# Expert weights in a ring of five places, and the last body's order

## The chip, the cores and the metric

The kernel runs on one core of one Trainium2 chip. Its time is the device time of one execution in microseconds, as the median of several. A separate execution was recorded by the hardware profiler; all durations below come from that one.

## The reference, cut to what matters

One decoder layer on 512 tokens of width 1024, all in float32. First an attention branch and a gated linear attention branch are computed and merged into the residual stream `h`. The last stage, which the change touches, is a mixture of 32 experts, in 4 groups of 8; each token goes to the best two experts of its best group:

```
for g in range(N_GROUPS):
    hg = jax.nn.silu(jnp.einsum('nd,edf->nef', xn, w_gate[g])) * jnp.einsum('nd,edf->nef', xn, w_up[g])
    y = y + jnp.einsum('nef,efd->nd', hg * combine[:, g, :, None], w_down[g])
return h + y_ffn
```

Each expert has a gate matrix (1024 x 256), an up matrix (1024 x 256) and a down matrix (256 x 1024). Each of these 96 matrices is 1024 KB and is read from HBM once.

## The kernel before, in words

**The stages.** The first part of the kernel (up to about 403 us) computes both branches, the router and the choice of experts. Its order is a list written out by hand (`SCHEDULE`). Then comes the expert stage, a loop over rounds; with these inputs there is one round. A round has 8 bodies (`BODIES`), a body has two pairs of experts (side s = 0 and s = 1), so body i holds pairs 2i and 2i+1, that is experts 4i to 4i+3. Each expert gets 64 slots (`SLOT`) for tokens; the two experts of a pair sit side by side in the 128 partitions.

**TensorE's order in a body** (`for i in range(BODIES)` in the tensor block): the gate and up products of pair 2i (`expert_gate_up(i, 0, ...)`, line 1023), those of pair 2i+1, then the down products of the body before (`down(i - 1, n - 1)`, line 1037, both sides), the transposes of the hidden rows (`hidden`, line 1031), the transposes of the gathered rows of the next body (`row_transposes`, line 1017), and the scatter of the body before (`scatter`, line 1110: one-hot products that spread the rows into 8 banks, which VectorE adds to `h`). Bodies 0 and 1 differ: body 0 does its own down products and body 1 does none. Body 7, the last, starts with the down products of body 6, then its own gate and up products, then the scatter of body 6; it ends with its own down products and a last scatter (`last_scatter`, line 1048). ScalarE takes the silu (`hs`, line 1542) and copies the down products (`high_rows`, line 1533), VectorE multiplies (`hg`, line 1997) and subtracts (`low_rows`, line 1970).

**The weights in SBUF.** `w_pair[s]` holds for side s one pair: 2 experts x (gate, up, down). So gate and up of four experts and the down matrices of four experts have a place (96 KB of each partition). The 16 KB at the start of the arena hold in the stage before `xnT` (two buffers of 4 KB, the transposed rows for the router) and `xs` (two buffers of 4 KB, the scaled rows on their way to `rows_hbm`, from which GpSimd gathers the experts' rows); in the expert stage this space is unused.

**The queue of the weights.** All weights are loaded by SyncE (SP) with `dma_start`, in the order of its program, on one hardware queue. SP waits for the semaphore that frees a place (`s_gu[s]`: gate and up products of side s done; `s_down[s]`: down products done) and issues the loads of that pair. The order of the 1024 KB loads, counted as pieces from the first, is: 1 to 5 the gate and up of pair 0 and one down matrix of it (issued at 340 us, when the last merged rows are split); three stores of scaled rows; 6 to 10 the gate and up of pair 1 and one down of it; 11 its other down; the fourth store (`store_rows(NB - 1)`, 512 KB); 12 the other down of pair 0; then `bodies_after_first`: gate and up of pairs 2 and 3 (13 to 20), down of pair 2 (21, 22), gate and up of pairs 4 and 5 (23 to 30), down of pair 3 (31, 32). From body 2 on a body asks for 8 gate and up pieces and 4 down pieces: 33 to 44, 45 to 56, 57 to 68, 69 to 80. At the end come gate and up of pair 14 (81 to 84), down of pairs 12 and 13 (85 to 88), gate and up of pair 15 (89 to 92), down of pairs 14 and 15 (93 to 96). One semaphore per side counts gate and up loads (`s_wgu`), one per side the down loads (`s_wd`).

**The gathers.** For body j GpSimd waits (once) until the four stores of scaled rows have landed, then, body by body, for the row numbers of side s, and issues an indirect DMA on a queue of its own (line 2144).

Of the kernel before, what the change touches and what calls it, by code (L numbers as in the profile page):

```python
# [28 lines left out]
P = 128  # L29
NB = T // P  # L30
KT = D // P
# [7 lines left out]
NG, EPG, FF = 4, 8, 256  # L39
# [6 lines left out]
PAIRS = NE // 2  # L46
BODIES = PAIRS // 2


# [216 lines left out]
def layer_kernel(nc, x, meta_tokens, norm1_w, w_in, q_norm_w, k_norm_w, attn_sinks, gla_gate_up, gla_gate_bias,  # L266
                 gla_norm_w, w_attn_branch, w_gla_branch, w_out, norm2_w, router_rows, norm2_rows,
                 expert_w_gate, expert_w_up, expert_w_down, table, triangle, rows_hbm, out):
    with ExitStack() as ctx:
# [89 lines left out]
        def more(name, shape, dt=F32):  # L359
# [66 lines left out]
        w_pair = [at(f"w_pair{s}", WE + 6 * s * 8 * K1, [P, 2, 3, KT * FF]) for s in range(2)]  # L426
        we = [[[w_pair[s][:, j, i, :].rearrange("p (k n) -> p k n", k=k) for i, k in enumerate((KT, KT, 2))]
               for j in range(2)] for s in range(2)]
        onehot_r = at("onehot_r", WE + 40 * K1, [P, NB, 2 * P], F32R)
# [102 lines left out]
        s_ylo = sem2("y_lo_ready")  # L532
        s_wgu = sem2("gate_up_loaded")
        s_wd = sem2("down_loaded")
# [75 lines left out]
        def slots(j, s):  # L610

            c = 32 * (j % 2) + 16 * s
            return tiles[W_BANK][:, c:c + 8]

        def scatter_bank(i, u):
# [12 lines left out]
        def _(pe):  # L628
# [373 lines left out]
            with pe.Fori(0, rounds) as r:  # L1002
# [17 lines left out]
                def expert_gate_up(i, s, part):  # L1020
                    for k in range(4 * part, 4 * part + 4):
                        for j in range(2):
                            last = nc.tensor.matmul(tiles[GU_BANK[s]][j * SLOT:(j + 1) * SLOT, :].rearrange("p (f n) -> p f n", f=2),  # L1023
                                                    xgT[:, k, s * P + j * SLOT:s * P + (j + 1) * SLOT],
                                                    w_pair[s][:, j, 0:2, k * FF:(k + 1) * FF],
                                                    start=(k == 0), stop=(k == KT - 1))
                    return last
# [6 lines left out]
                def expert_down(s, half):  # L1034
                    for f in range(2):
                        for j in range(2):
                            last = nc.tensor.matmul(tiles[DOWN_BANKS[s][half]][j * SLOT:(j + 1) * SLOT, :],  # L1037
                                                    hT[s][:, f, j * SLOT:(j + 1) * SLOT],
                                                    we[s][j][2][:, f, half * 512:(half + 1) * 512],
                                                    start=(f == 0), stop=(f == 1))  # L1040
                    return last
# [73 lines left out]
                for i in range(BODIES):  # L1115
                    n = r * BODIES + i

                    if i + 1 == BODIES:
                        down(i - 1, n - 1)
                    pe.wait_ge(s_xgT[0], n + 1)  # L1120
                    pe.wait_ge(s_wgu[0], 64 * n + 64)
                    expert_gate_up(i, 0, 0)
                    pe.wait_ge(s_xgT[1], n + 1)
                    expert_gate_up(i, 0, 1).then_inc(s_gu[0], 1)
                    if i == 0:
                        first_slot_weights()
                        for s in range(2):
                            pe.wait_ge(s_ohT[s], n + 1)
                        onehot_transposes(1)
                    pe.wait_ge(s_xgT[2], n + 1)  # L1130
                    pe.wait_ge(s_xgT[3], n + 1)
                    pe.wait_ge(s_wgu[1], 64 * n + 64)
                    expert_gate_up(i, 1, 0)
# [46 lines left out]
        def _(sp):  # L1180
# [17 lines left out]

            def load(pair, s, gate_up, slots=(0, 1)):
                for j in slots:  # L1200
                    e = pair * 2 + j
                    for i, w in ((0, expert_w_gate), (1, expert_w_up)) if gate_up else ((2, expert_w_down),):
                        src = w[0].rearrange("g e a n -> (g e) a n")[bass.ds(e, 1), :, :]
                        src = src.rearrange("o (p k) n -> p (o k) n", p=P) if gate_up else \
                            src.rearrange("o (k p) n -> p (o k) n", p=P)
                        sp.dma_start(we[s][j][i][:, :, :], src).then_inc((s_wgu if gate_up else s_wd)[s], 16)

            def next_gate_up(i, n, sides=(0, 1)):

                for s in sides:  # L1210
                    sp.wait_ge(s_gu[s], n)
                    load(2 * i + s, s, True)

            def next_down(i, n, sides=(0, 1)):

                for s in sides:
                    sp.wait_ge(s_down[s], n)
                    load(2 * i + s, s, False)

            def bodies_after_first(n):  # L1220

                next_gate_up(1, n + 1)
                next_down(1, n + 1, (0,))
                next_gate_up(2, n + 2)
                next_down(1, n + 1, (1,))
                with sp.Fori(2, BODIES - 2) as i:
                    next_gate_up(i + 1, n + i + 1)
                    next_down(i, n + i)
                last = BODIES - 1
                next_gate_up(last, n + last, (0,))  # L1230
                next_down(last - 1, n + last - 1)
                next_gate_up(last, n + last, (1,))
                next_down(last, n + last)

            sp.wait_ge(s_mlo, KT)
            load(0, 0, True)
            load(0, 0, False, (0,))
            def store_rows(b):
# [5 lines left out]
            sp.wait_ge(*banks.emptied(("unit", WO + 1, NB - 1)))  # L1244
            load(1, 1, True)
            load(1, 1, False, (0,))
            sp.wait_ge(s_sq2, 4 * NB)
            load(1, 1, False, (1,))
            store_rows(NB - 1)
            sp.wait_ge(s_pick[3], 1)  # L1250
            sp.wait_ge(s_cast, 2)
            load(0, 0, False, (1,))
            bodies_after_first(0)
            sp.wait_ge(s_rounds, 1)
            rounds = sp.value_load(rounds_i[0:1, 0:1], min_val=1, max_val=T // SLOT)
            with sp.If(rounds > 1):
                with sp.Fori(1, rounds) as r:
                    next_gate_up(0, r * BODIES)
                    next_down(0, r * BODIES)
                    bodies_after_first(r * BODIES)  # L1260
            for u in range(2 * NB):
# [8 lines left out]
        def _(act):  # L1270
# [252 lines left out]
            with act.Fori(0, rounds) as r:  # L1523
# [12 lines left out]
                for i in range(BODIES):  # L1536
                    n = r * BODIES + i
                    if i + 1 == BODIES:
                        high_rows(n - 1)
                    for s in range(2):  # L1540
                        act.wait_ge(s_gu[s], n + 1)
                        nc.scalar.activation(hs[s][:, :], tiles[GU_BANK[s]][:, 0:FF], ACT.Silu).then_inc(s_silu[s], 1)  # L1542
                        if s == 0 and i == 0:
                            onehot_out(1, n + 1)
# [19 lines left out]
        def _(dve):  # L1564
# [371 lines left out]
            with dve.Fori(0, rounds) as r:  # L1936
# [52 lines left out]
                for i in range(BODIES):  # L1989
                    n = r * BODIES + i  # L1990
                    if i + 1 == BODIES:
                        low_rows(n - 1)
                    dve.wait_ge(s_pw, n + 1)
                    for s in range(2):
                        dve.wait_ge(s_silu[s], n + 1)

# [206 lines left out]
```

## Time and profile before

| | us |
|---|---|
| median of 3 runs (663.23 to 665.02) | 663.85 |
| the profiled execution, its own time | 663.98 |
| its span, first to last instruction | 662.2 |
| TensorE busy in the span | 639.2 (97%) |
| hardware queue q1, share of 16 DMA engines over the span | 53.3% |

The span is shorter than the time by 1.8 us, which lie before the first and behind the last instruction. Busy shares are means over stages: the expert stage is the last 259 us, and it is the only one in which the DMA engines are full. TensorE's granted clock is 0.997 of full speed over the span, so no stage of it runs at the lower level.

### The profile page before, as it was taken

How to read it: one execution, taken by the hardware profiler on the slowest of the kernel's cores; microseconds unless marked ns; L12 is line 12 of the kernel's file. 1: busy time of each engine (PE TensorE's matmuls, PEld its weight loads, DVE VectorE, ACT ScalarE, POOL GpSimd, SP SyncE). 2: the span in 40 equal slices, each digit the busy share in tenths (PEclk: the TensorE clock that was granted, in tenths of full speed). 3: DMA queues.
4: the chain of work that ended last, by engine and by line, in shares of the span. 5: the costliest groups of instructions: out<-in, count | busy, mean ns of one | idle time of the engine just before them, and what ended most of it. 6: DMA issues, size and time to landing. Idle time of an engine off the chain costs nothing.

```text
span 662.2 us, 10015 instructions
## 1 busy us (share of the span) xinstructions
PE 639.2 (97%) x3887; PEld 461.9 (70%) x3887; DVE 390.9 (59%) x721; ACT 213.7 (32%) x436; POOL 110.7 (17%) x168
## 2 busy tenths in 40 slices
PE   5799999999999999999989999999999999999998
PEld 3579999998787878778789996345454454635355
DVE  4648335688997979776674667435253443526145
ACT  6346222224444343422534565200101010111112
POOL 3300006799500000000000010111010101010001
PEclk9899999999999999999999999999999999999999
DMA  7442222302232221111454067999999999999933
GB/s 248 150 127 65 64 65 70 120 4 64 65 89 82 83 64 66 64 64 63 149 194 198 33 257 287 419 414 413 418 410 419 409 421 410 420 410 414 414 128 127
DMA packets 49794, 138.78 MB, mean 210 GB/s; under 512 B 6202, under 2 KB 28235, under 8 KB 41556
## 3 DMA queue, kind: packets, MB, share of 16 engines
q1 hardware_dynamic: 47298, 134.44, 53.3%
q0 software_dynamic: 2304, 3.64, 1.5%
q8 instruction: 31, 0.51, 0.3%
q14 instruction: 15, 0.12, 0.1%
q10 hardware_dynamic: 146, 0.07, 0.0%
HBM read 138.69 MB, written 4.19 MB: 216 GB/s over the span
## 4 chain that ended last, share of the span: by engine, by line
PE 85%; DMA 6%; DVE 4%; ACT 2%; issue 2%; POOL 0%; SPq 0%; ACTq 0%; DVEq 0%
PE bank L1023 16%; PE bank L632 13%; PE bank L633 12%; PE bank L634 12%; PE bank L1037 8%; PE bank L1110 6%; DMA w_pair<-in_expert_w_up 3%; DMA w_pair<-in_expert_w_down 2%; PE bank L1017 1%; PE bank L874 1%; PE bank L976 1%; PE bank L1048 1%; PE bank L907 1%; PE bank L942 1%; ACT whi L1313 1%
## 5 line engine op out<-in xcount | busy, mean ns | idle before, releaser
L1023 PE MATMUL bank<-w_pair,xgT 128*64 128x512 f32 x512 | 112.0, 594 | 1.6 <-DMA w_pair<-in_expert_w_up 1.6
L1023 PEld LDWEIGHTS bank<-w_pair,xgT 128*64 128x64 f32 x512 | 37.3, 137 | 70.0 <-issue 69.2
L1635 DVE TENSOR_TENSOR wlo<-wraw,whi 128x2048 fp32r<-128x2048 f32 (+1 forms) x25 | 56.4, 2257 | 20.0 <-ACT whi L1313 20.0
L632 PE MATMUL bank<-whi,xhi 128*128 128x256 f32 x224 | 64.4, 288 | 0.0
L634 PE MATMUL bank<-whi,xlo 128*128 128x256 f32 x224 | 62.9, 281 | 0.0
L633 PE MATMUL bank<-wlo,xhi 128*128 128x256 f32 x224 | 62.9, 281 | 0.0
L632 PE MATMUL bank<-xhi,whi 128*128 128x512 f32 x152 | 62.3, 410 | 0.0
L1037 PE MATMUL bank<-w_pair,hT 128*64 128x512 f32 x256 | 56.7, 593 | 4.2 <-DMA w_pair<-in_expert_w_down 3.1
L633 PE MATMUL bank<-xlo,whi 128*128 128x512 f32 x152 | 60.1, 395 | 0.0
L634 PE MATMUL bank<-xhi,wlo 128*128 128x512 f32 x152 | 59.7, 393 | 0.0
L1997 DVE SCALAR_TENSOR_TENSOR hg<-bank,pair_w,hs 128x256 f32<-128x256 f32 x16 | 7.7, 484 | 84.0 <-ACT hs L1542 84.0
L1313 ACT ACTIVATE whi<-wraw 128x2048 fp32r<-128x2048 f32 (+1 forms) x25 | 46.7, 1872 | 24.9 <-PE bank L641 11.1
L1982 DVE TENSOR_TENSOR h<-h,bank 128x512 f32<-128x512 f32 x64 | 42.0, 683 | 9.6 <-PE bank L1110 8.2
L1970 DVE TENSOR_TENSOR y_lo<-bank,y_hi 128x512 fp32r<-128x512 f32 x32 | 20.6, 686 | 44.7 <-ACT y_hi L1533 44.7
L1037 PEld LDWEIGHTS bank<-w_pair,hT 128*64 128x64 f32 x256 | 18.8, 137 | 39.4 <-issue 37.2
L2036 POOL TENSOR_TENSOR pause<-pause 128x1 f32<-128x1 f32 x34 | 8.8, 270 | 222.8 <-PE bank L1017 119.6
L1110 PE MATMUL bank<-y_hi,onehotT 128*128 128x512 f32 x112 | 44.3, 396 | 0.0
L1110 PE MATMUL bank<-y_lo,onehotT 128*128 128x512 f32 x112 | 43.7, 390 | 0.0
L632 PEld LDWEIGHTS bank<-whi,xhi 128*128 128x128 f32 x224 | 42.1, 188 | 1.8 <-issue 1.4
L634 PEld LDWEIGHTS bank<-whi,xlo 128*128 128x128 f32 x224 | 42.2, 188 | 0.0
L633 PEld LDWEIGHTS bank<-wlo,xhi 128*128 128x128 f32 x224 | 42.1, 188 | 0.0
L1542 ACT ACTIVATE hs<-bank 128x256 f32<-128x256 f32 x16 | 6.1, 383 | 99.5 <-PE bank L1023 99.5
(333 smaller groups left out, 1301.9 us busy)
## 6 DMA issues: line engine op xcount, KB each, us to landing
w_pair<-in_expert_w_gate SPq DMA_DIRECT2D x32, 1024.0 KB
w_pair<-in_expert_w_up SPq DMA_DIRECT2D x32, 1024.0 KB
w_pair<-in_expert_w_down SPq DMA_DIRECT2D x32, 1024.0 KB, 20.4
wraw<-in_w_in SPq DMA_DIRECT2D x17, 1024.0 KB, 5.5
wraw<-in_w_out SPq DMA_DIRECT2D x4, 1024.0 KB, 5.1
h<-in_x SPq DMA_DIRECT2D x4, 512.0 KB, 5.1
wraw<-in_w_gla_branch SPq DMA_DIRECT2D x2, 1024.0 KB, 5.2
wraw<-in_w_attn_branch SPq DMA_DIRECT2D x2, 1024.0 KB, 5.1
```

What stands on the lines that cost most here:

```text
L632: nc.tensor.matmul(ps, lhi(k), rhi(k), start=(k == 0), stop=False)
L633: nc.tensor.matmul(ps, lhi(k), rlo(k), start=False, stop=False)
L634: last = nc.tensor.matmul(ps, llo(k), rhi(k), start=False, stop=(k == kt - 1))
L1023: last = nc.tensor.matmul(tiles[GU_BANK[s]][j * SLOT:(j + 1) * SLOT, :].rearrange("p (f n) -> p f n", f=2), xgT[:, k, s * P + j * SLOT:s * ...
L1037: last = nc.tensor.matmul(tiles[DOWN_BANKS[s][half]][j * SLOT:(j + 1) * SLOT, :], hT[s][:, f, j * SLOT:(j + 1) * SLOT], we[s][j][2][:, f, ...
L1110: last = nc.tensor.matmul(scatter_bank(i, u)[:, :], onehotT[i % 3][s][:, b, :], part[s][:, cols_], start=(s == 0 and part is y_hi), stop=( ...
L1313: nc.scalar.activation(wh, raw, ACT.Copy).then_inc(s_hi, 1)
L1635: nc.vector.tensor_tensor(wl, raw, wh.bitcast(F32), ALU.subtract).then_inc(s_lo, 1)
L1970: last = nc.vector.tensor_tensor(y_lo[s][:, cols_], tiles[DOWN_BANKS[s][half]][:, :], y_hi[s][:, cols_].bitcast(F32), ALU.subtract)
L1982: nc.vector.tensor_tensor(h[:, b, cols_], h[:, b, cols_], scatter_bank(i, u)[:, :], ALU.add).then_inc(s_add[u % 4], 1)
L1997: nc.vector.scalar_tensor_tensor(hg[s][:, :], tiles[GU_BANK[s]][:, FF:2 * FF], pair_w[:, 2 * i + s:2 * i + s + 1], hs[s][:, :], ALU.mult, ...
L2036: return nc.gpsimd.tensor_tensor(o, a, b, op)
```

## The change

Gate and up move out of `w_pair` into a ring of five places (`w_ring`): four are the gate and up parts of `w_pair`, the fifth is `w_fifth`, 16 KB at the start of the arena. Expert e goes to place e % 5, each place has a semaphore of its own, and a pair waits for its two experts' places. The down matrices stay where they were. After the gate and up products of pair p SP loads experts 2p+5 and 2p+6. The order of SP's program changes with it: expert 4's gate is issued behind the last logits and ahead of the fourth store, its up behind a wait for the third and fourth store to land; in body 0 both pairs of down matrices (2 and 3) are asked for ahead of the gate and up of pairs 4 to 6; in body 7 nothing but down matrices is left to load. The loop on SP is unrolled.

In body 7 TensorE does the gate and up products of pair 14 ahead of the down products of body 6; ScalarE's `high_rows` and VectorE's `low_rows` of body 6 move between the two sides accordingly.

```diff
--- before.py
+++ after.py
@@ -45,6 +45,7 @@
+RING = 5
@@ -424,8 +425,9 @@
         y_lo = [more(f"y_lo{i}", [P, D], F32R) for i in range(2)]
         assert place[0] <= 80 * K1, place[0] / K1
         w_pair = [at(f"w_pair{s}", WE + 6 * s * 8 * K1, [P, 2, 3, KT * FF]) for s in range(2)]
-        we = [[[w_pair[s][:, j, i, :].rearrange("p (k n) -> p k n", k=k) for i, k in enumerate((KT, KT, 2))]
-               for j in range(2)] for s in range(2)]
+        wd = [[w_pair[s][:, j, 2, :].rearrange("p (k n) -> p k n", k=2) for j in range(2)] for s in range(2)]
+        w_fifth = at("w_fifth", 0, [P, 2, KT * FF])
+        w_ring = [w_pair[s][:, j, 0:2, :] for s in range(2) for j in range(2)] + [w_fifth[:, :, :]]
         onehot_r = at("onehot_r", WE + 40 * K1, [P, NB, 2 * P], F32R)
         assert WE + 44 * K1 <= G + 48 * K1
         def view(t, rows, groups):
@@ -530,7 +532,7 @@
         s_down = sem2("down_done")
         s_yhi = sem2("y_hi_ready")
         s_ylo = sem2("y_lo_ready")
-        s_wgu = sem2("gate_up_loaded")
+        s_ring = [sem(f"gate_up{k}_loaded") for k in range(RING)]
         s_wd = sem2("down_loaded")
         s_sc = [sem(f"scatter_bank{i}_full") for i in range(4)]
         s_add = [sem(f"scatter_bank{i}_added") for i in range(4)]
@@ -611,6 +613,10 @@
 
             c = 32 * (j % 2) + 16 * s
             return tiles[W_BANK][:, c:c + 8]
+
+        def ring_loads(n, e):
+
+            return 32 * (n * len(range(e % RING, NE, RING)) + e // RING + 1)
 
         def scatter_bank(i, u):
 
@@ -1022,7 +1028,7 @@
                         for j in range(2):
                             last = nc.tensor.matmul(tiles[GU_BANK[s]][j * SLOT:(j + 1) * SLOT, :].rearrange("p (f n) -> p f n", f=2),
                                                     xgT[:, k, s * P + j * SLOT:s * P + (j + 1) * SLOT],
-                                                    w_pair[s][:, j, 0:2, k * FF:(k + 1) * FF],
+                                                    w_ring[(4 * i + 2 * s + j) % RING][:, :, k * FF:(k + 1) * FF],
                                                     start=(k == 0), stop=(k == KT - 1))
                     return last
 
@@ -1036,7 +1042,7 @@
                         for j in range(2):
                             last = nc.tensor.matmul(tiles[DOWN_BANKS[s][half]][j * SLOT:(j + 1) * SLOT, :],
                                                     hT[s][:, f, j * SLOT:(j + 1) * SLOT],
-                                                    we[s][j][2][:, f, half * 512:(half + 1) * 512],
+                                                    wd[s][j][:, f, half * 512:(half + 1) * 512],
                                                     start=(f == 0), stop=(f == 1))
                     return last
 
@@ -1115,13 +1121,14 @@
                 for i in range(BODIES):
                     n = r * BODIES + i
 
-                    if i + 1 == BODIES:
-                        down(i - 1, n - 1)
                     pe.wait_ge(s_xgT[0], n + 1)
-                    pe.wait_ge(s_wgu[0], 64 * n + 64)
+                    for e in (4 * i, 4 * i + 1):
+                        pe.wait_ge(s_ring[e % RING], ring_loads(r, e))
                     expert_gate_up(i, 0, 0)
                     pe.wait_ge(s_xgT[1], n + 1)
                     expert_gate_up(i, 0, 1).then_inc(s_gu[0], 1)
+                    if i + 1 == BODIES:
+                        down(i - 1, n - 1)
                     if i == 0:
                         first_slot_weights()
                         for s in range(2):
@@ -1129,7 +1136,8 @@
                         onehot_transposes(1)
                     pe.wait_ge(s_xgT[2], n + 1)
                     pe.wait_ge(s_xgT[3], n + 1)
-                    pe.wait_ge(s_wgu[1], 64 * n + 64)
+                    for e in (4 * i + 2, 4 * i + 3):
+                        pe.wait_ge(s_ring[e % RING], ring_loads(r, e))
                     expert_gate_up(i, 1, 0)
                     expert_gate_up(i, 1, 1).then_inc(s_gu[1], 1)
                     if 2 <= i < BODIES - 1:
@@ -1196,45 +1204,51 @@
             for c in range(2, NCHUNK):
                 load_w(c)
 
-            def load(pair, s, gate_up, slots=(0, 1)):
+            def rows_of(w, e, **by):
+                return w[0].rearrange("g e a n -> (g e) a n")[e, :, :].rearrange(by.pop("as_"), **by)
+
+            def load_gate(e, both=True):
+                sp.dma_start(w_ring[e % RING][:, 0, :].rearrange("p (k n) -> p k n", k=KT),
+                             rows_of(expert_w_gate, e, as_="(p k) n -> p k n", p=P)).then_inc(s_ring[e % RING], 16)
+                if both:
+                    load_up(e)
+
+            def load_up(e):
+                sp.dma_start(w_ring[e % RING][:, 1, :].rearrange("p (k n) -> p k n", k=KT),
+                             rows_of(expert_w_up, e, as_="(p k) n -> p k n", p=P)).then_inc(s_ring[e % RING], 16)
+
+            def load_down(pair, slots=(0, 1)):
                 for j in slots:
...
-            def next_gate_up(i, n, sides=(0, 1)):
-
-                for s in sides:
-                    sp.wait_ge(s_gu[s], n)
-                    load(2 * i + s, s, True)
-
...
-            def bodies_after_first(n):
-
-                next_gate_up(1, n + 1)
-                next_down(1, n + 1, (0,))
-                next_gate_up(2, n + 2)
-                next_down(1, n + 1, (1,))
-                with sp.Fori(2, BODIES - 2) as i:
-                    next_gate_up(i + 1, n + i + 1)
-                    next_down(i, n + i)
-                last = BODIES - 1
-                next_gate_up(last, n + last, (0,))
-                next_down(last - 1, n + last - 1)
-                next_gate_up(last, n + last, (1,))
-                next_down(last, n + last)
+                    sp.dma_start(wd[pair % 2][j][:, :, :],
+                                 rows_of(expert_w_down, 2 * pair + j, as_="(k p) n -> p k n", p=P)).then_inc(s_wd[pair % 2], 16)
+
+            def next_gate_up(pair, n):
+
+                sp.wait_ge(s_gu[pair % 2], n + pair // 2 + 1)
+                for e in (2 * pair + RING, 2 * pair + RING + 1):
+                    if e < NE:
+                        load_gate(e)
+
+            def next_down(pair, n):
+
+                sp.wait_ge(s_down[pair % 2], n + pair // 2 + 1)
+                load_down(pair + 2)
+
+            def rest_of_round(n):
+
+                for i in range(BODIES):
+                    for pair in (2 * i, 2 * i + 1):
+                        if pair + 2 < PAIRS:
+                            next_gate_up(pair, n)
+                    if i != 1:
+                        done = i if i == 0 else i - 1
+                        for pair in (2 * done, 2 * done + 1):
+                            next_down(pair, n)
 
             sp.wait_ge(s_mlo, KT)
-            load(0, 0, True)
-            load(0, 0, False, (0,))
+            for e in range(2):
+                load_gate(e)
+            load_down(0, (0,))
             def store_rows(b):
                 sp.wait_ge(s_xs_loc[b], 1)
                 sp.dma_start(rows_hbm[b * P:(b + 1) * P, :], xs[b % 2][:, :]).then_inc(s_xsd[b], 16)
@@ -1242,22 +1256,33 @@
             for b in range(NB - 1):
                 store_rows(b)
             sp.wait_ge(*banks.emptied(("unit", WO + 1, NB - 1)))
-            load(1, 1, True)
-            load(1, 1, False, (0,))
+            for e in range(2, 4):
+                load_gate(e)
+            load_down(1, (0,))
             sp.wait_ge(s_sq2, 4 * NB)
-            load(1, 1, False, (1,))
+            load_down(1, (1,))
+            sp.wait_ge(*banks.filled(("logits", NB - 1)))
+            load_gate(4, False)
             store_rows(NB - 1)
             sp.wait_ge(s_pick[3], 1)
             sp.wait_ge(s_cast, 2)
-            load(0, 0, False, (1,))
-            bodies_after_first(0)
+            load_down(0, (1,))
+            for b in (NB - 2, NB - 1):
+                sp.wait_ge(s_xsd[b], 16)
+            load_up(4)
+            rest_of_round(0)
...
@@ -1535,9 +1560,9 @@
 
                 for i in range(BODIES):
                     n = r * BODIES + i
-                    if i + 1 == BODIES:
-                        high_rows(n - 1)
                     for s in range(2):
+                        if s == 1 and i + 1 == BODIES:
+                            high_rows(n - 1)
                         act.wait_ge(s_gu[s], n + 1)
                         nc.scalar.activation(hs[s][:, :], tiles[GU_BANK[s]][:, 0:FF], ACT.Silu).then_inc(s_silu[s], 1)
                         if s == 0 and i == 0:
@@ -1988,10 +2013,10 @@
                 next_onehots(2)
                 for i in range(BODIES):
                     n = r * BODIES + i
-                    if i + 1 == BODIES:
-                        low_rows(n - 1)
                     dve.wait_ge(s_pw, n + 1)
                     for s in range(2):
+                        if s == 1 and i + 1 == BODIES:
+                            low_rows(n - 1)
                         dve.wait_ge(s_silu[s], n + 1)
 
                         nc.vector.scalar_tensor_tensor(hg[s][:, :], tiles[GU_BANK[s]][:, FF:2 * FF], pair_w[:, 2 * i + s:2 * i + s + 1],
```

## Rows read from the trace of the kernel before

**Rows 1.** DMA and engines by stretch; last columns granted clock, DMA share, GB/s.
```profile
389.00:404.00 15.00, 14.88 (x129) 14.48 (x130) 11.97 (x36) 10.11 (x24) 2.40 (x3) 1.00 1.01 410
404.00:408.00 4.00, 4.00 (x20) 1.29 (x18) 3.44 (x19) 3.80 (x10) 0.00 (x0) 1.00 0.94 328
408.00:413.00 5.00, 5.00 (x44) 2.05 (x42) 2.90 (x12) 1.47 (x3) 0.39 (x2) 1.00 0.27 68
413.00:463.00 50.00, 47.40 (x260) 22.18 (x256) 21.97 (x50) 7.09 (x16) 8.60 (x16) 1.00 1.02 416
463.00:600.00 137.00, 136.85 (x716) 67.46 (x718) 56.39 (x116) 19.77 (x43) 13.09 (x24) 1.00 1.02 415
600.00:630.00 30.00, 26.90 (x134) 14.32 (x130) 11.88 (x19) 4.19 (x9) 0.19 (x1) 1.00 1.02 413
```
**Rows 2.** Who waited for whom on TensorE: us in total, times, longest.
```profile
PE bank L1037 <- DMA w_pair<-in_expert_w_down: 3.1, 2, 1.6
PE bank L1023 <- DMA w_pair<-in_expert_w_up: 1.6, 1, 1.6
```
**Rows 3.** TensorE's instructions in body 2 and the start of body 3.
```profile
454.48 7.09 PE L1023 MATMUL bank<-w_pair,xgT 128*64 128x512 f32 x32
463.15 7.09 PE L1023 MATMUL bank<-w_pair,xgT 128*64 128x512 f32 x32 [1.58 <-DMA w_pair<-in_expert_w_up]
...
487.31 13.95 PE L1023 MATMUL bank<-w_pair,xgT 128*64 128x512 f32 x64
```
**Rows 4.** TensorE's instructions at the end of body 6 and in body 7.
```profile
594.27 7.04 PE L1037 MATMUL bank<-w_pair,hT 128*64 128x512 f32 x32
...
612.51 3.65 PE L1037 MATMUL bank<-w_pair,hT 128*64 128x512 f32 x16 [1.57 <-DMA w_pair<-in_expert_w_down]
617.70 3.65 PE L1037 MATMUL bank<-w_pair,hT 128*64 128x512 f32 x16 [1.53 <-DMA w_pair<-in_expert_w_down]
```
**Rows 5.** The chain of work that ended last, pieces from 445 us on.
```profile
445.63 17.38 DMA w_pair<-in_expert_w_up
...
601.76 15.80 DMA w_pair<-in_expert_w_down
...
621.35 13.73 PE bank L1023 x64
...
643.72 7.02 PE bank L1037 x32
```
**Rows 6.** SP's DMA issues, start and length, 388 to 447 us.
```profile
388.50 6.21 SPq L1206 DMA_DIRECT2D w_pair<-in_expert_w_down  x2
401.35 0.34 SPq L1240 DMA_DIRECT2D rows_hbm<-xs  x1
403.40 0.37 SPq L1206 DMA_DIRECT2D w_pair<-in_expert_w_down  x1
410.89 0.34 SPq L1206 DMA_DIRECT2D w_pair<-in_expert_w_gate  x1
...
425.10 1.48 SPq L1206 DMA_DIRECT2D w_pair<-in_expert_w_down  x2
446.11 0.94 SPq L1206 DMA_DIRECT2D w_pair<-in_expert_w_down  x2
```
**Rows 7.** Landing of the fourth store (the issue at 401.35).
```profile
DMA to landing us min/median/max: 6.4/6.4/6.4
```
**Rows 8.** Landing of pieces 31 and 32 (the issues from 446.11 on).
```profile
DMA to landing us min/median/max: 20.2/21.3/22.3
```
**Rows 9.** DMA in one microsecond, as the weights' queue starts again.
```profile
412.00:413.00 1.00, 1.00 (x6) 0.29 (x4) 0.84 (x6) 0.93 (x2) 0.19 (x1) 1.00 0.42 115
```
**Rows 10.** GpSimd around the first gather.
```profile
408.96 0.19 POOL L2036 TENSOR_TENSOR pause<-pause 128x1 f32<-128x1 f32 x1 [13.57 <-issue]
412.51 0.19 POOL L2036 TENSOR_TENSOR pause<-pause 128x1 f32<-128x1 f32 x1 [3.36 <-DVE row_no L1621]
```
**Rows 11.** VectorE's part of the copies of body 6's second down products.
```profile
622.02 1.29 DVE L1970 TENSOR_TENSOR y_lo<-bank,y_hi 128x512 fp32r<-128x512 f32 x2 [3.89 <-ACT y_hi L1533]
```

More of the change, by code:

```diff
@@ L1197, in _ @@
                 load_w(c)
-            def load(pair, s, gate_up, slots=(0, 1)):
-                for j in slots:
[L1201 to L1206, printed above, removed]
@@ L1208, in next_gate_up @@
-            def next_gate_up(i, n, sides=(0, 1)):
-                for s in sides:
-                    sp.wait_ge(s_gu[s], n)
-                    load(2 * i + s, s, True)
[L1214 to L1218, printed above, removed]
-            def bodies_after_first(n):
-                next_gate_up(1, n + 1)
-                next_down(1, n + 1, (0,))
-                next_gate_up(2, n + 2)
-                next_down(1, n + 1, (1,))
-                with sp.Fori(2, BODIES - 2) as i:
-                    next_gate_up(i + 1, n + i + 1)
-                    next_down(i, n + i)
-                last = BODIES - 1
-                next_gate_up(last, n + last, (0,))
-                next_down(last - 1, n + last - 1)
-                next_gate_up(last, n + last, (1,))
-                next_down(last, n + last)
+            def rows_of(w, e, **by):
+                return w[0].rearrange("g e a n -> (g e) a n")[e, :, :].rearrange(by.pop("as_"), **by)
@@ L1257, in _ @@
                 with sp.Fori(1, rounds) as r:
-                    next_gate_up(0, r * BODIES)
-                    next_down(0, r * BODIES)
-                    bodies_after_first(r * BODIES)
+                    for pair in range(2):
+                        sp.wait_ge(s_gu[pair], r * BODIES)
+                        sp.wait_ge(s_down[pair], r * BODIES)
+                    for e in range(RING):
+                        load_gate(e)
+                    for pair in range(2):
+                        load_down(pair)
+                    rest_of_round(r * BODIES)
             for u in range(2 * NB):
```

## The prediction

> **What bounds the kernel now.** I read four views in this order. The windows come first [rows 1]: from 413 us until 630 us the DMA engines are full (share 1.02, 413 to 416 GB/s) while TensorE is almost always busy too, so the expert stage has two limits lying close together. Then the waits [rows 2]: TensorE waited for weights only three times in the whole stage, 4.7 us in all. The timeline gives their places: 1.58 us ahead of the gate and up products of pair 5 in body 2 [rows 3], and 1.57 and 1.53 us ahead of the two down products of body 6, at the start of body 7 [rows 4]. The chain [rows 5] says which loads they waited for: piece 30 (issued 445.63, landed 463.01) and piece 88 (issued 601.76, landed 617.56). Between them lie 58 pieces in 154.6 us, 2.66 us each, gathers included. A body asks for 12 pieces, so 31.9 us of transfers, and TensorE takes 31.0 us for one: body 3 starts at 487.31 and the down products behind the gate and up products of body 6 at 594.27, which is 13.9 us into it, so three bodies take 93.1 us [rows 3, 4]. TensorE runs away from the weights by 0.9 us in each body, lives on a lead, and pays at both ends. What counts is therefore not how many places there are but how many pieces stand in the queue ahead of the one that TensorE wants, and how much time the engines lose before they fill.
>
> Between 404 and 413 us they lose time: shares of 0.94 over 4 us and 0.27 over 5 us leave 3.9 us idle [rows 1].
>
> **The change part by part.**
>
> *The fifth place, filled early.* Expert 4's gate (a piece, 1.05 MB, 2.53 us at 415 GB/s) is issued at about 394.7 us, right behind piece 11 [rows 6], and goes into the idle stretch whole. It pushes the fourth store, which landed at 401.35 + 6.4 = 407.75 us [rows 6, 7], to about 410.3. Only then does SP issue the up. Before, the queue started again at 410.89 [rows 6]; now it starts again at 410.3, 0.6 us sooner. The engines are at their full rate about 2.1 us after an issue (share 0.42 in the microsecond from 412 [rows 9], and full from 413 [rows 1], after the issue at 410.89). On average the engines stopped at 413 - 3.9 = 409.1; with the gate they stop at 411.6 and are full again at 412.4, so 0.8 us of the idle time stays. All later pieces come 3.9 - 0.8 = 3.1 us sooner than the same count did. I call this the lead. Its lower end is the gate alone, 2.5 us; its upper end is the 3.9 us of idle time, or 5.1 us if both pieces went into the slack whole.
>
> The Trainium skill, page "DMA: Bandwidth & Descriptors", section "Specifications", puts the first byte of an SP-issued transfer at about 0.6 us. By that the up would flow before the queue runs dry and the lead would be 3.9 us; the trace does not agree, since the share is still 0.42 more than a microsecond after the issue.
>
> *What stands behind the new waits.* Behind SP's wait for the stores stand the up of expert 4 (needed at 430 us) and the loads that `s_gu[0]` frees at about 410.85 us. That is 0.5 us after my landing time, so the wait costs nothing; if the store lands later, every microsecond takes one from the lead. GpSimd waits for the same store: it went on at 408.96, and then stood until 412.51 for a row number [rows 10]. Moved by 2.5 us it goes on at 411.5, so the first gather does not move.
>
> *Body 2.* Its order of loads is different: the downs of pair 3 (pieces 31, 32 before) now stand ahead of the gate and up of pairs 4 and 5, because both pairs' downs are asked for in body 0 at 425.1 us and some 3.4 us later. The ring adds two pieces more for the expert that is ahead, but expert 11, which pair 5 needs, is complete with piece 32 (10 gate and up and 4 down pieces at first, 8, 4, then 6 for experts 9 to 11). Piece 32 landed at 446.58 + 22.3 = 468.9 us [rows 8]. With the lead it lands at 465.8, against 463.01 for piece 30 before. So the first stall does not go, it grows from 1.58 to 4.4 us: **+2.8 us**. Pair 4 needs piece 28: 463.0 - 5.3 - 3.1 = 454.6, just when TensorE wants it (454.5).
>
> *Bodies 3 to 6.* The requests keep the queue full: at 461.5 us 34 pieces are asked for and 31 landed. TensorE's loss of 0.9 us a body is covered by the slack that its later start gives. The last of these to matter is piece 82 (down of pair 11): about 617.56 - 6 x 2.6 - 3.1 = 598.9, needed at 594.27 + 2.8 + 3.5 = 600.6. No stall, 1.7 us to spare.
>
> *Body 7.* Scatter 5 ends at 612.51 - 1.57 = 610.94, now 613.7. The gate and up of pair 14 (landed long before) take 6.9 us, until 620.6, and cover what was the first down stall. Down 12 is complete with piece 90: 617.56 + 5.1 - 3.1 = 619.5, in time (2.54 us a piece at 413 GB/s, without gathers). Its products end at 624.1. Down 13 is complete with piece 92, since all gate and up of pair 15 now stand ahead of it: 617.56 + 4 x 2.54 - 3.1 = 624.6. TensorE waits 0.6 us, resumes at about 624.8, does 3.65 us of down and 6.9 us of gate and up products, and starts scatter 6 at 635.3. Before it started at 621.35 + 13.73 = 635.1 [rows 5]. Four pieces more (10.2 us) minus half of the gate and up products moved ahead (6.8 us) minus the lead (3.1 us): **+0.3 us**, or +0.2 by the clock times. By TensorE's own path alone it is +2.8 - 1.57 - 1.53 = -0.3, so the two bounds meet within 0.5 us.
>
> *The rest.* The copies of body 6's down products (VectorE's part ends 2.0 us after the products do [rows 5, 11]) lay beside 13.7 us of products and now lie beside 6.9 us: still covered, and if they weren't, the scatter would start up to 2 us late. The last silu and product stay where they were relative to the scatter's first two banks. Down 14 is asked for at 624.1 and lands near 632, down 15 at 628 and lands near 638; needed at 643.7 and 647.2 [rows 5]. Twice as many semaphore waits on TensorE: 16 more instructions, which its sequencer takes ahead of running matmuls (64 products in 13.95 us with such waits in the middle, two times 32 in 7.09 us each without [rows 3]); between 0 and 0.5 us in all, and I take 0. Nothing behind 635 us changes.
>
> The sum is +0.2 us on the profiled execution's 663.98 us (span 662.2 and 1.8 around it). That execution is 0.13 us above the median of 663.85, so the forecast for the median is **664.0 us**.
>
> **The rivals.**
>
> *A, the lead is larger.* If the engines which end last never run dry (they are still at work while the mean share is falling), the lead is 3.9 to 5.1 us. For: the landing time of the slowest engine sets the semaphore, and rows 9 show a mean only. Against: the restart at 410.3 still takes 2.1 us. Time: the sum moves one for one, 3.3 - 3.9 = -0.6 to 3.3 - 5.1 = -1.8: 662.0 to 663.3 us.
>
> *B, the stalls go.* If the downs of pair 3 don't hold up pair 5 (TensorE not waiting in body 2), and body 7's stalls go too: -1.58 - 1.57 - 1.53 = -4.7, 659.2 us. For: it is what a ring with more room would give if TensorE were the limit. Against: rows 1 and 5; it would want a lead of 7.5 us, with only 3.9 us idle.
>
> *C, slower.* The store lands late, because it stands behind the gate on engines that lag, and SP's wait holds back all loads freed at 410.85. From a landing at about 411.5 on the lead falls below 2 us; landing at 413 leaves 0.5 us, and the sum is 3.3 - 0.5 = +2.8 us: 666.6 us. It decides from a lead below 1.2 us, where the sum passes +2 us. For: nothing in the old trace shows how far the store slips. Against: before, it landed 6.4 us after its issue with the rest of pieces 10 and 11 ahead of it, as their sizes ask.
>
> *D, the moved downs turn into a new wait elsewhere in bodies 3 to 6.* TensorE's margin there is 1.7 us; with a piece at 2.73 us rather than 2.66 it is gone, but such a wait only brings forward what body 7 waits for. Within +0.5 us: part of the forecast's own range.
>
> **How the numbers follow.** Forecast with D: 0.60, its own range 663.2 to 665.0. A: 0.19. B: 0.07. C: 0.14. The range of 8 in 10 leaves out B and the far half of C: 661.6 to 665.8 us. A measurement of this kernel tells 0.3%, 2.0 us, from no change, so faster means below 661.9 and slower above 665.8. Faster: B and a tenth of the rest, where more than one of my small terms is off, 0.16. Slower: C's far half and a little of the forecast, 0.12. Same: 0.72.
>
> **What would show it.** Right: DMA share near 1 from 389 until past 408 us, a short dip near 412; one stall of about 4 us in body 2, at pair 5, or split over pairs 4 and 5; none in bodies 3 to 6; body 7 with gate and up products at 613.7, a stall under 1.5 us ahead of the second down only; scatter 6 near 635 us. Wrong: no stall in body 2 (B), or a first gather issued later than 414 us and a queue idle past 413 us (C).

## The result and the profile after

| | before | changed |
|---|---|---|
| median us (13 executions each) | 663.82 (663.22 to 665.02) | 666.02 (664.70 to 667.83) |
| ratio, 95% interval | | 1.0034 (1.0026 to 1.0043) |
| profiled execution, span | 662.2 | 665.5 |
| TensorE's mean granted clock in it | 0.997 | 0.990 |

The change costs 2.2 us. The forecast was 664.0 us and the range 661.6 to 665.8; the time lies 0.2 us outside it, and slower by more than 0.3% had a chance of 0.12. The profiled execution of the changed kernel took 667.33 us and is the second slowest of its 13, so its trace shows more loss than the medians do.

The first view is the windows of the changed kernel, in the columns of [rows 1]: start and end, length, busy us (and instructions) of TensorE, its weight loads, VectorE, ScalarE and GpSimd, then TensorE's granted clock, the DMA share and GB/s.

```profile
404.00:408.00 4.00, 4.00 (x26) 1.66 (x27) 3.58 (x17) 3.95 (x11) 0.00 (x0) 1.00 1.00 355
408.00:413.00 5.00, 5.00 (x44) 2.05 (x42) 2.91 (x12) 1.38 (x4) 0.19 (x1) 1.00 0.88 325
413.00:463.00 50.00, 48.25 (x264) 22.48 (x260) 22.27 (x55) 7.85 (x18) 8.82 (x17) 1.00 1.01 415
463.00:600.00 137.00, 133.07 (x684) 65.45 (x686) 55.07 (x114) 18.31 (x40) 13.09 (x24) 0.98 1.01 410
```

The idle stretch is filled but for a dip (0.88 where 0.27 stood), as forecast. What was not forecast stands in the last column but two of the last row: a granted clock of 0.98 over 137 us. In finer windows it has a place:

```profile
463.00:466.90 3.90, 0.00 (x0) 0.00 (x1) 0.44 (x1) 0.00 (x0) 0.00 (x0) 0.90 1.03 414
...
468.00:472.00 4.00, 4.00 (x12) 1.16 (x10) 0.00 (x0) 0.00 (x0) 0.00 (x0) 0.50 1.01 420
472.00:473.00 1.00, 1.00 (x6) 0.34 (x4) 0.00 (x0) 0.00 (x0) 0.00 (x0) 0.54 1.03 426
473.00:474.00 1.00, 1.00 (x8) 0.40 (x6) 0.00 (x0) 0.00 (x0) 0.00 (x0) 1.00 1.02 426
```

TensorE stands from 462.4 to 466.9 us, its clock falls near the end of that wait to the lower level (0.50, 1.2 GHz), and it is at full speed again from 473 us. The instructions of pair 5 in body 2 show the price, start and length in the first two columns, to be held against the second of [rows 3] (the trace lists each float32 product of the program as two instructions, so 16 products stand as x32):

```profile
466.93 10.05 PE L1029 MATMUL bank<-w_pair,xgT 128*64 128x512 f32 x32 [4.51 <-DMA w_pair<-in_expert_w_up]
```

The wait is 4.51 us (1.58 before) and the same x32 instructions take 10.05 us instead of 7.09. The chain of work that ended last (start, length, what) gives the rest; it answers to [rows 5]:

```profile
445.53 21.26 DMA w_pair<-in_expert_w_up
...
617.67 7.02 PE bank L1029 x32
...
631.55 6.87 PE bank L1029 x32
638.42 2.04 PE bank L1116 x8
```

Body 7 runs without any wait, and scatter 6 starts at 638.4 where it started at 635.1.

**The account.** Of the 3.3 us between the two spans, 0.84 us lie ahead of the expert stage (body 0 starts at 404.67 instead of 403.83) and are not put down to the change: TensorE's clock at the start of the kernel differs from execution to execution. From 20 to 25 us it is 0.66 in the profiled execution before and 0.50 in the changed one. So the sentence ahead of the prediction that a mean of 0.997 leaves no stage at the lower level is wrong. The kernel before alone shows the spread: in the three later sets of runs, its executions with a mean clock of 0.997 have medians of 663.5 to 663.6 us (20, 15 and 8 of them), those with 0.995 medians of 664.5, 664.8 and 664.6 (7 each). The rest is 4.51 - 1.58 = +2.9 us of wait, 10.05 - 7.09 = +3.0 us of slow products, and -3.4 us in body 7 (two waits of 1.57 and 1.53, and 0.3 us at the two restarts): +2.5 us, against 2.2 between the medians.

### The profile page after: what moved, and what is told of

Its sections match the earlier page's. It is cut to its first block, busy times and chain, and to the rows that moved or that the text cites. A ratio compares the mean times of both kernels' runs of the same rounds, so it can differ in the third digit from the quotient of the medians.

```text
span 665.5 us, 9939 instructions
## 1 busy us (share of the span) xinstructions
PE 643.3 (97%) x3887; PEld 462.7 (70%) x3887; DVE 391.1 (59%) x721; ACT 213.7 (32%) x436; POOL 110.7 (17%) x168
## 4 chain that ended last, share of the span: by engine, by line
PE 87%; DMA 4%; DVE 4%; ACT 2%; issue 2%; POOL 0%; ACTq 0%; SPq 0%; DVEq 0%
PE bank L1029 16%; PE bank L638 12%; PE bank L639 12%; PE bank L640 12%; PE bank L1043 8%; PE bank L1116 7%; DMA w_pair<-in_expert_w_up 3%; PE bank L1023 2%; PE bank L880 1%; PE bank L982 1%; PE bank L1054 1%; PE bank L913 1%; PE bank L948 1%; ACT whi L1338 1%; DVE sig_a L1730 1%
## 5 line engine op out<-in xcount | busy, mean ns | idle before, releaser
L1029 PE MATMUL bank<-w_pair,xgT 128*64 128x512 f32 x416 | 115.2, 610 | 4.5 <-DMA w_pair<-in_expert_w_up 4.5
L1029 PE MATMUL bank<-w_fifth,xgT 128*64 128x512 f32 x96 | 42.4, 594 | 0.0
```

## The experiments

**One part undone: the order of pair 3's down matrices.**

```
-                    if i != 1:
-                        done = i if i == 0 else i - 1
-                        for pair in (2 * done, 2 * done + 1):
-                            next_down(pair, n)
+                    if i == 0:
+                        next_down(0, n)
+                    elif i == 1:
+                        next_down(1, n)
+                    else:
+                        for pair in (2 * i - 2, 2 * i - 1):
+                            next_down(pair, n)
```

> The changed kernel with one thing undone: pair 3's down matrices are asked for behind the gate and up of pairs 4, 5 and 6's first expert, as before. Theory 1 (the order of the loads makes the 4.5 us stall of body 2, and the stall puts TensorE's clock down, which costs 3.0 us more): experts 10 and 11 are complete two pieces (5.3 us) sooner, so no stall ahead of pair 5 in body 2, its 32 products take 7.0 us, no clock below 1 there. TensorE then catches up with the weights in body 7 and waits some 3.2 us ahead of down 12 and 1.5 us ahead of down 13. Time 664.0 us, 2 below the changed kernel, the same as before; if the 3.2 us wait also lowers the clock, up to 667. Rival 2 (the products that read the ring are slow for another reason, such as the fifth place's address or transfers into it): pair 5 still takes 10 us and the time stays at 666.

Measured 663.95 us, ratio to before 1.0005 (0.9995 to 1.0014). No wait and no fall of the clock in body 2: the gate and up products of pairs 4 and 5 are one block of 13.88 us. The waits came elsewhere than written down: one each in bodies 5, 6 and 7, each ahead of the second pair's down products, where 3.2 and 1.5 us had been expected in body 7 alone. From TensorE's waits:

```profile
PE bank L1043 <- DMA w_pair<-in_expert_w_down: 4.3, 3, 1.5
```

The chain shows scatter 6 at 634.43 us, 0.7 us ahead of the kernel before, of which 0.45 us lie ahead of the expert stage. So the stall is the order's. That the time is what I had forecast for the change is chance: it is made up of other waits.

**The wait filled, the weights no sooner.**

```
+                    if i == 2:
+                        for _ in range(5):
+                            nc.tensor.matmul(tiles[GU_BANK[1]][:, :], ident, cst[:, P:P + 512], start=True, stop=True)
                     for e in (4 * i + 2, 4 * i + 3):
                         pe.wait_ge(s_ring[e % RING], ring_loads(r, e))
```

> The changed kernel with five more products (identity by 512 columns of the constants, into the bank that pair 5 is about to overwrite) ahead of the wait for pair 5's weights in body 2. The result doesn't change. Theory 1: they fill most of the 4.5 us stall, the weights come no sooner, but the clock stays at full speed and pair 5 takes 7.0 rather than 10.05 us. Scatter 6 is then set by the weights of down 13: 3 us less minus a new wait of about 0.6 us in body 7, so 663.6 to 664.4 us. Rival 2 (slow products for another reason than idle time): pair 5 still takes 10 us, time 666 or more.

Measured 663.78 us, ratio 1.0002 (0.9993 to 1.0011), 2.2 us below the changed kernel. Its instructions (the five products stand as x10):

```profile
462.07 4.56 PE L1141 MATMUL bank<-cst 128*128 128x512 f32 x10
466.56 7.09 PE L1029 MATMUL bank<-w_pair,xgT 128*64 128x512 f32 x32
```

Counted from the start of body 0, pair 5 starts within 0.1 us of where it starts in the changed kernel, and it takes 7.09 us. The weights, their places and the transfers beside them are the same; only TensorE's idleness is gone. This rules out that the ring's address or the traffic into it slows the products. Filling the idle time alone brings back the whole 2.2 us; the longer wait (+2.9) is paid back in body 7 (-3.4).

**The other part undone: body 7's order.** TensorE, ScalarE and VectorE do body 7 as before:

```
+                    if i + 1 == BODIES:
+                        down(i - 1, n - 1)
                     pe.wait_ge(s_xgT[0], n + 1)
...
                     expert_gate_up(i, 0, 1).then_inc(s_gu[0], 1)
-                    if i + 1 == BODIES:
-                        down(i - 1, n - 1)
```

> The changed kernel with body 7 in its old order on TensorE, ScalarE and VectorE: the down products of body 6 ahead of pair 14's gate and up. Theory 1 (body 7's new order is a gain, the loss lies in body 2): down 13 is complete only at about 625 us, and 3.65 + 13.7 us of products then stand ahead of scatter 6, which starts at about 642 instead of 637.6 us: 670 us, 4 above the changed kernel; if the wait lowers the clock, up to 673. Rival 3 (moving the copies of body 6 between the two sides and the products ahead is what costs the 2 us): 664 us.

Measured 671.19 us, ratio 1.0115 (1.0100 to 1.0131). In its body 7 TensorE waits twice:

```profile
619.54 3.65 PE L1043 MATMUL bank<-w_pair,hT 128*64 128x512 f32 x16 [3.00 <-DMA w_pair<-in_expert_w_down]
624.70 3.65 PE L1043 MATMUL bank<-w_pair,hT 128*64 128x512 f32 x16 [1.51 <-DMA w_pair<-in_expert_w_down]
```

and scatter 6 starts at 642.1 us, as written down (the 670 us beside it were 1 us short: 28.9 us follow that point in the kernel before). Body 2 is as in the changed kernel, with a wait of 4.54 us and 9.67 us for pair 5. Once the gate and up of pair 15 stand ahead of down 12 and 13 in the queue, body 7's new order is worth 5 us; it is needed, not harmful. The 3.00 us wait left the clock at 1.00.

**The parts put into the kernel before, one at a time.** Pair 3's downs early:

```
-                next_down(1, n + 1, (0,))
+                next_down(1, n + 1)
                 next_gate_up(2, n + 2)
-                next_down(1, n + 1, (1,))
```

> The kernel before with pair 3's down matrices asked for ahead of the gate and up of pairs 4 and 5, and nothing else changed: that part of the change alone, without ring and lead. Theory 1: pair 5 of body 2 is complete with piece 32 at 468.3 to 468.9 us, a stall of 6.9 to 7.4 us instead of 1.58, and the clock falls behind it: 3.0 us more. TensorE then is so late that the two stalls of body 7 (3.1 us) go: 5.6 + 3.0 - 3.1 = +5.5, 669.3 us. Without a clock loss 666.3 us. Rival 2 (it is the ring's place that makes products slow): no product slower than before, 666.

Measured 666.72 us, ratio 1.0043 (1.0028 to 1.0057). The stall is split over both pairs of body 2, and both are slow after it:

```profile
457.56 8.78 PE L1023 MATMUL bank<-w_pair,xgT 128*64 128x512 f32 x32 [3.09 <-DMA w_pair<-in_expert_w_up]
468.94 8.48 PE L1023 MATMUL bank<-w_pair,xgT 128*64 128x512 f32 x32 [2.59 <-DMA w_pair<-in_expert_w_up]
```

5.7 us of wait and 1.7 + 1.4 us of slow products, without ring and without fifth place: the order alone makes the stall and the fall of the clock. The sum was 2.6 us too high. The wait was put down 1.5 us too long (6.9 to 7.4 us instead of 5.7), and the slow products, 3.1 us here, are those of an execution of 667.95 us, 1.2 us above its median.

The last body's order alone, in the kernel before (the diff of the change without its SP part):

> The kernel before with only the last body's order changed (pair 14's gate and up ahead of body 6's down products). Theory 1: both stalls ahead of the downs go, since their weights land at 612.4 and 617.6 us; the gate and up of pair 15 is then complete only at about 627.7 us, TensorE waits some 3 us for it and starts scatter 6 at 634.7 instead of 635.1 us. Time 663.4 us, the same as before; if the 3 us wait lowers the clock, 666.

Measured 664.68 us, ratio 1.0011 (1.0002 to 1.0020). The wait moved as written down, with 2.40 us in place of 3 (the clock stayed at 1.00 in it):

```profile
628.34 7.09 PE L1023 MATMUL bank<-w_pair,xgT 128*64 128x512 f32 x32 [2.40 <-DMA w_pair<-in_expert_w_up]
```

All 11 executions have a mean clock of 0.995, and the profiled one lost it at the start of the kernel (0.50 between 20 and 25 us, 0.66 in the kernel before). Its expert stage starts 0.83 us later (404.66 against 403.83), and from there to scatter 6 it is 0.5 us quicker, where 0.4 us was written down. So in this execution the loss stands ahead of the part that was changed, and the changed part is as forecast. Why this kernel always starts so is open.

**What the early gate is worth.** First the gate moved to the up's place, behind the stores' landing:

```
-            sp.wait_ge(*banks.filled(("logits", NB - 1)))
-            load_gate(4, False)
             store_rows(NB - 1)
...
-            load_up(4)
+            load_gate(4)
```

> The changed kernel with expert 4's gate issued where its up is, behind the wait for the stores, so that nothing fills the idle stretch ahead of 413 us. Theory 1 (the early gate gives a lead of 3.1 us, the queue is served in order): the fourth store lands at about 407.8 as before, the queue starts again there with two pieces, a lead of 2 to 3 us instead of 3.1 (the restart comes 3 us sooner, with nothing of the idle stretch filled by the gate). So nearly the same stall in body 2, 4.5 to 5.5 us, same clock loss of 3 us, time 666 to 667. If the early gate is what counts, the stall is 7 us and the time 668.5 us.

Measured 665.41 us, ratio 1.0021 (1.0008 to 1.0034); the wait in body 2 is 4.1 us, no longer than with the early gate, where a wait of 7 us was written down for the case that the early gate counts. SP issued the gate at 408.42 and the share of the stretch from 408 to 413 us is 0.90 without an early gate, 0.88 with it. So the gate that "goes into the idle stretch whole" is a push, not a gain: it delays the store by 2.5 us, and with it the restart. Then the gate between the two, behind the store's issue but not behind its landing:

```
-            load_gate(4, False)
             store_rows(NB - 1)
+            load_gate(4, False)
```

> The changed kernel with the fourth store issued ahead of expert 4's gate instead of behind it, nothing else. Theory 1: the store lands at about 407.8 us as before, the up of expert 4 is issued then, with the gate and the down matrix still in the queue, so the engines lose nothing between 404 and 413 us (share 1.0) and the lead grows from 3.1 to between 3.9 and 5 us. Body 2's stall shrinks by as much, from 4.5 to between 2.6 and 3.7 us; the clock may still fall behind it. Body 7 is then bound by down 13 as forecast. Time 663 us without a fall of the clock, 665 to 666 with one. If the idle stretch was worth nothing (rival: the lead comes from the ring's place alone), the stall stays at 4.1 to 4.5 us.

Measured 662.77 us, ratio 0.9987 (0.9972 to 1.0002), not told apart from the kernel before, in ten executions from 661.4 to 666.3. The idle stretch is gone, and the wait is 2.90 us:

```profile
404.00:408.00 4.00, 4.00 (x20) 1.29 (x18) 3.44 (x19) 3.72 (x9) 0.00 (x0) 1.00 1.01 402
408.00:413.00 5.00, 5.00 (x45) 2.06 (x43) 2.91 (x13) 1.47 (x3) 0.39 (x2) 1.00 1.04 389
...
464.40 8.78 PE L1029 MATMUL bank<-w_pair,xgT 128*64 128x512 f32 x32 [2.90 <-DMA w_pair<-in_expert_w_up]
```

Piece 32 lands 4.6 us sooner than in the kernel before (464.27 against 468.9). Moving one line is worth 3.3 us against the changed kernel.

**A better order.** On top of down3_late, expert 31 goes behind down 12 and 13:

```
-                        if pair + 2 < PAIRS:
+                        if pair + 3 < PAIRS:
                             next_gate_up(pair, n)
...
                         for pair in (2 * i - 2, 2 * i - 1):
                             next_down(pair, n)
+                    if i == BODIES - 2:
+                        next_gate_up(PAIRS - 3, n)
```

> The changed kernel with two changes of the order of SP's loads only: pair 3's down matrices behind the next gate and up as in down3_late, and the last expert's gate and up (31) behind the down matrices of pairs 12 and 13 instead of ahead. Theory 1: no stall in body 2; down 13 is complete with piece 90 at about 619.5 us, where TensorE wants it at 619.8; expert 31 is complete with piece 92 at 624.6 us, TensorE waits about 1.5 us for it and then has 6.9 us of products ahead of scatter 6, which starts at 631.6 us rather than 635.1 us in the kernel before: 660.4 us, faster than both kernels by 0.5% or more. Rival 2 (slow products from the ring): 663 or more.

Measured 662.40 us, ratio 0.9981 (0.9972 to 0.9990), 2 us above what I wrote down. Three waits of 3.1 us in all, ahead of the second pair's down products in bodies 4 to 6, had been left out of the sum. They are the same question again, what stands ahead in the queue, so the next kernel moved the pieces that are wanted last:

```
                    late = []
                    for pair in (2 * i, 2 * i + 1):
                        if pair + 2 < PAIRS:
                            sp.wait_ge(s_gu[pair % 2], n + pair // 2 + 1)
                            for e in (2 * pair + RING, 2 * pair + RING + 1):
                                if e == 4 * i + 8 or e == NE - 1:
                                    late += [e] if e < NE else []
                                else:
                                    load_gate(e)
                    for pair in ((0,), (1,))[i] if i < 2 else (2 * i - 2, 2 * i - 1):
                        next_down(pair, n)
                    for e in late:
                        load_gate(e)
```

> best_order with one change more: in every body the gate and up of expert 4i+8, which TensorE wants only two bodies later, stand behind the down matrices and not ahead of them. Theory 1 (served in order, late is what stands behind too many pieces): the three waits of 1 to 1.5 us for the second down matrices in bodies 4 to 6 (3.1 us in all in best_order) go, since these are complete 5.3 us sooner. TensorE reaches body 7 3.1 us sooner and waits some 1.5 us for expert 31, complete at about 624.6 us: scatter 6 at 631.6 us, time 660.5 us, 0.5% faster than before. If the queue runs dry because the requests come later, 662 or more.

Measured 660.95 us, ratio 0.9952 (0.9938 to 0.9965). What is left of the waits for weights, beside one of 0.2 us for a down matrix:

```profile
PE bank L1029 <- DMA w_pair<-in_expert_w_up: 1.4, 1, 1.4
```

And the gate behind the fourth store's issue on top of it, by the same edit as in store_first:

> last_gates_late with the fourth store issued ahead of expert 4's gate. Theory 1: the lead grows by 1 to 2 us, which shortens the one wait that is left, 1.4 us ahead of expert 31's pair in body 7. Scatter 6 starts at about 631 instead of 632 us: 659.7 to 660.4 us against 660.95. If the idle stretch is worth nothing: 661 us.

Measured 659.80 us, ratio 0.9932 (0.9919 to 0.9946). One wait for weights is left, and in the profiled execution the clock stays at 1.00 through the stage:

```profile
PE bank L1029 <- DMA w_pair<-in_expert_w_up: 0.3, 1, 0.3
```

This kernel beats the one before by 3.9 us and the changed one by 6.2 us. It is the change with nothing but the order of its loads corrected. No run has this order without the fifth place, so how much of the 3.9 us is the ring's is not shown.

## Why the prediction was wrong

*What bounds the kernel, and the pieces' order:* right. Piece 32 was to land at 465.8 us and to make a stall of 4.4 us; it landed at 466.79, that is 465.95 by the clock of the first execution, with 4.51 us. The fourth store was to land at 410.3; it was issued at 402.25 and took 8.9 us, 410.3 less the same shift.

*The lead of 3.1 us:* right in size (468.9 - 465.95 = 2.95), wrong in its cause, so the agreement is luck. late_gate has it without the early gate. It comes from asking before 410.85 us; the early gate only takes the store's turn. The sum also took the lost time from the busy shares, 3.9 us. By the bytes it is 5.0 us: 328 and 68 GB/s over 4 and 5 us in [rows 1], held against 415. The same count leaves 1.7 us lost in the changed kernel (355 and 325 GB/s), 1.6 in late_gate (379 and 310) and 0.4 in store_first (402 and 389). The gains of 3.4, 3.4 and 4.6 us stand beside leads of 2.95, 3.1 and 4.6 us. The first two lose another 0.3 to 0.4 us in the microsecond from 413 us (336 and 295 GB/s, against 467 before).

*Body 2, "it grows from 1.58 to 4.4 us: +2.8 us":* this step failed. The wait was priced at its own length, and the products behind it at full speed, without a reason given. The expert stage of before held three waits of at most 1.58 us, all with the clock at 1.00 behind them, and I carried that to one of 4.4 us. It cost 4.51 - 1.58 = 2.9 us and another 3.0 us in the products behind it. The Trainium skill, page "TensorE: Matmul & The Clock Gate", section "HAM oscillation — how this bites in real kernels", describes this: TensorE waits for a transfer, the chip lowers its clock, and the next group of products starts at the lower level. The trace agrees (0.50 from 466.9 to 472 us). That belonged among the rivals, with a time of 664.0 + 2.2 to 3.0; busy_wait is the forecast without it, and measured 663.78.

The trace of before held the warning, in its first 25 us (two of TensorE's instructions with the wait ahead of each, then two windows with busy us, granted clock, DMA share and GB/s):

```profile
10.64 4.35 PE L714 MATMUL bank<-cst,xr 128*128 128x128 f32 x24 [4.14 <-DVE xr L1646]
20.43 3.52 PE L660 MATMUL bank<-xhi,gdp 128*48 128x512 f32 x8 [3.92 <-DVE xlo L1653]
...
5.00:15.00 10.00, 5.86 (x26) 1.00 1.01 323
20.00:25.00 5.00, 4.57 (x13) 0.66 0.78 237
```

Behind a wait of 4.14 us the clock is at 1.00, behind one of 3.92 us it falls. A wait of 4.4 us was therefore one that might cost the clock, and its price had to be a range.

*Body 7, bound by down 13:* the wait of 0.6 us did not come, in the changed kernel or in busy_wait, where TensorE is late by the 2.9 us of the wait alone. So TensorE's own path sets the end in both, and the slow products count in full: from the start of body 0 to scatter 6 the changed kernel takes 233.75 us and busy_wait 230.74. In busy_wait scatter 6 starts at 635.11 us, or 634.5 us less the 0.6 us by which this execution is late at body 2, where the sum said 635.3.

*Bodies 3 to 6:* no wait in the changed kernel, as forecast. The margin is under 4.9 us: down3_late, which reaches body 3 at 485.2 us where the forecast had 490.1, waits in bodies 5 and 6. The 1.7 us of the sum was not measured.

*Rival C* had the right sign by a wrong mechanism: the store did not land late, and no load freed at 410.85 was held back.

## What to carry to other kernels

When transfers are served in order and are the limit, count for every wait the pieces in the queue up to the one wanted; here a deeper ring gained nothing while the same edit put other pieces ahead of it. Price a wait of TensorE that is longer than those seen to be harmless twice: once for its length, once for the products behind it at half the clock. Count lost transfer time in bytes, not in busy share. And when a small transfer releases others, issue it ahead of the bulk, not behind it.

## What the runs showed of the hardware that was not expected

Whether a wait lowers the clock, and for how long, did not follow from its length alone. Behind waits of 1.5 to 1.8 us it stayed at 1.00, and so it did behind 2.40 and 3.00 us in body 7 and behind 4.14 us at the start of the kernel before; it fell behind 2.59, 2.90, 3.09, 4.1, 4.51 and 4.54 us in body 2, and behind 3.92 us at the start. The slow products of body 2 then cost between 1.4 us (before_down3_early, late_gate) and 3.0 us. With the same kernel it varies as well: the changed kernel's 13 executions have mean clocks of 0.990, 0.992 and, once, 0.995, and store_first, with a wait of 2.9 us, ran from 661.4 us (mean 0.997) to 666.3 us (0.992). What decides it between 2.4 and 4.2 us was not settled.

The engines' share rises within a microsecond of an issue (0.53 in the microsecond from 411 us, after one at 410.89), but the bytes don't: 66, 115 and then 467 GB/s in the microseconds from 411, 412 and 413 us of the kernel before. The prediction held its figure for the first byte against the share of 0.42 from 412 us and found no agreement. The 0.53 of the microsecond before shows transfers under way within 1.1 us of the issue; what came late was the full rate, so that reading went too far.
